# Two-block network on one core: the three engines' order of work in the twelve head pairs of the state-space scan

## The reference, cut to what matters

```python
def ssd_chunked(x, dt, A, B, C, h0):           # cut
    a_cum = jnp.cumsum(a, axis=-1)
    lmat = jnp.exp(segsum(a))                   # decay from token s to token l, one matrix a head
    cb = jnp.einsum('bclgn,bcsgn->bgcls', cc, bc)
    y_diag = jnp.einsum('bgcls,bgrcls,bcsgrp->bclgrp', cb, lmat, xc)
    ...
    y_off = jnp.einsum('bclgn,bcgrpn,bgrcl->bclgrp', cc, prev_states, jnp.exp(a_cum))
    y = (y_diag + y_off).reshape(bsz, length, g, r, p)

def ssd_mixer(...):                             # cut: forward and backward scan, skip, gate, norm by group
    y = y_f + flip(y_b) + d_skip * xs
    gated = y * jax.nn.silu(zs)
    gated = gated * lax.rsqrt(jnp.mean(gated * gated, axis=-1, keepdims=True) + EPS)

# beside it, for the second block: adaptive scales, shifts and gates from a conditioning vector
mods = jnp.split(silu_c @ ada_w[l] + ada_b[l], 6, axis=-1)
```

## Time and profile before

| | |
|---|---|
| three timed runs | 2001.25, 2004.65, 2007.44 us |
| profiled execution | 2007.44 us, span on the core 2005.4 us |
| PE busy | 1729.2 us, 86% of the span |
| DVE, ACT, POOL busy | 619.6, 356.7, 56.2 us |
| granted PE clock, mean | 0.945 of full speed |
| the twelve pairs | from 298.25 us (first `head_rows`) to 425.65 us (first product of `w_out0`), 127.4 us |

### The profile page before, as it was taken

The page is one execution under the profiler, slowest core; times in us unless marked ns, Lnnn a source line. Parts: engine busy times, 40 slices in busy tenths (PEclk is TensorE's granted clock), DMA queues, the critical chain, the costliest instruction groups (busy, mean ns, idle before and its releaser), DMA issues.

```text
span 2005.4 us, 23465 instructions
## 1 busy us (share of the span) xinstructions
PE 1729.2 (86%) x9806; PEld 881.8 (44%) x9806; DVE 619.6 (31%) x1405; ACT 356.7 (18%) x868; POOL 56.2 (3%) x51
## 2 busy tenths in 40 slices
PE   6999998899999998989999989889998766566664
PEld 3844674444444576433333323246574433233322
DVE  2157837633200485332222222140343101110101
ACT  2112226512101363100000000021441000000000
POOL 0000200020100000000000000000000000000000
PEclk9899998899999999999999999999999977888887
DMA  8241337786322103279999999941307999999996
GB/s 335 105 168 48 121 126 284 296 340 258 121 84 84 42 1 126 103 298 429 427 428 428 427 427 426 428 175 53 142 35 305 423 427 427 427 426 427 427 427 254
DMA packets 39100, 538.21 MB, mean 268 GB/s; under 512 B 4330, under 2 KB 4714, under 8 KB 6612
## 3 DMA queue, kind: packets, MB, share of 16 engines
q1 hardware_dynamic: 37860, 530.84, 63.9%
q0 software_dynamic: 1136, 5.88, 0.8%
HBM read 535.66 MB, written 1.05 MB: 268 GB/s over the span
## 4 chain that ended last, share of the span: by engine, by line
PE 58%; issue 25%; DMA 11%; DVE 5%; ACT 1%; DVEq 1%; POOL 0%; SPq 0%; POOLq 0%; ACTq 0%
PE bank L597 55%; DMA mem<-in_moe 8%; PE bank L607 2%; DVE mem L1326 1%; DMA mem<-in_w_ada 1%; DVEq L1323 1%; DMA mem<-in_w_out 1%; DMA mem<-in_ada_w 0%; POOL mem L2303 0%; DVE mem L1489 0%; DVE mem L1800 0%; ACT mem L2009 0%; DVE mem L1617 0%; ACT mem L1990 0%; DVE mem L1638 0%
## 5 line engine op out<-in xcount | busy, mean ns | idle before, releaser
L597 PE MATMUL bank<-mem 128*32 128x256 f32 (+12 forms) x8990 | 1612.5, 495 | 251.5 <-DMA mem<-in_moe 162.3
L597 PEld LDWEIGHTS bank<-mem 128*32 128x32 f32 (+4 forms) x8990 | 790.5, 150 | 1019.0 <-issue 715.4
L2009 ACT ACTIVATE mem<-bank 128x512 f32<-128x512 f32 (+3 forms) x285 | 142.5, 507 | 1096.7 <-PE bank L597 767.9
L1800 DVE TENSOR_TENSOR mem<-mem,bank 128x512 f32<-128x512 f32 (+1 forms) x32 | 17.7, 554 | 490.8 <-PE bank L597 490.8
L1817 DVE TENSOR_TENSOR mem<-bank,mem 32x512 f32<-32x512 f32 (+1 forms) x128 | 70.9, 554 | 227.3 <-PE bank L597 226.0
L607 PE MATMUL bank<-mem 128*128 128x128 f32 x760 | 120.3, 287 | 16.1 <-DVE mem L1800 5.2
L607 PEld LDWEIGHTS bank<-mem 128*128 128x128 f32 x760 | 88.3, 147 | 80.6 <-issue 46.7
L1463 DVE SCALAR_TENSOR_TENSOR mem<-mem 128x256 f32<-128x256 f32 x160 | 86.9, 543 | 9.6
L1990 ACT ACTIVATE mem<-mem 128x1024 f32<-128x1024 f32 x22 | 23.1, 1051 | 190.4 <-DVE mem L1557 147.4
L1326 DVE TENSOR_SCALAR mem<-bank,mem 128x128 f32<-128x128 f32 (+2 forms) x136 | 45.4, 405 | 35.5 <-PE bank L607 31.7
L1964 ACT ACTIVATE mem<-bank 128x256 f32<-128x256 f32 (+2 forms) x54 | 19.7, 396 | 169.9 <-PE bank L597 169.9
(11 more groups left out here) (181 smaller groups left out, 515.1 us busy)
## 6 DMA issues: line engine op xcount, KB each, us to landing
mem<-in_moe SPq DMA_DIRECT2D x192, 2048.0 KB, 34.9
mem<-in_ada_w SPq DMA_DIRECT2D x24, 2048.0 KB, 8.2
mem<-in_w_in SPq DMA_DIRECT2D x10, 2048.0 KB, 7.6
mem<-in_w_ada SPq DMA_DIRECT2D x6, 2048.0 KB, 12.3
mem<-in_even_w_in SPq DMA_DIRECT2D x6, 2048.0 KB, 10.2
mem<-in_w_out SPq DMA_DIRECT2D x4, 2048.0 KB, 8.9
mem<-in_odd_w_in SPq DMA_DIRECT2D x3, 2048.0 KB, 21.0
mem<-in_even_w_out SPq DMA_DIRECT2D x2, 2048.0 KB, 8.2
```

The costliest lines, as they stand in the source:

```text
L597: return nc.tensor.matmul(o, lhsT, rhs, start=start, stop=stop, skip_group_check=True)
L2009: took(name, S.activation(o, i, func))
```

## The change

The order in which PE, DVE and ACT take the steps of the twelve pairs is written anew. No instruction is added or removed, and no buffer is changed.

- PE: iteration m now ends with `pair_y(m)` instead of holding `pair_y(m - 1)` in its middle. The two `head_rows` of the next pair stand apart, each with one adaptive row behind it. `ada_outs` comes one row after its own row, where before it came an iteration later. Sums and group rows follow one iteration nearer.
- DVE: `pair_out(m - 1)` stands before the second `decay_args` and before `mixing(m)`, where before it stood behind `mixing(m)`. In the pairs that close a group (m = 5, 8, 11), `group_ms` stands ahead of both `decay_args`.
- ACT: a `take` of an adaptive row follows each `decays`, and `pair_squares(m - 1)` is last.

```diff
-            for m in range(HEADS // 2 + 1):
-
-                for h in (2 * m + 2, 2 * m + 3):
-                    if h < HEADS:
-                        head_rows(h)
-                if m:
-                    pair_y(m - 1)
-                if m >= 3:
-                    pair_sum(m - 3)
...
-                for k in pending:
-                    ada_outs(k)
-                pending = [ADA_AT_HEAD[h] for h in (2 * m, 2 * m + 1) if h in ADA_AT_HEAD]
-                for k in pending:
-                    ada_rows(k)
+            for m in range(HEADS // 2):
+                for h in (2 * m, 2 * m + 1):
+                    if h + 2 < HEADS:
+                        head_rows(h + 2)
+                    if h in ADA_AT_HEAD:
+                        ada_rows(ADA_AT_HEAD[h])
+                        if h:
+                            ada_outs(ADA_AT_HEAD[h] - 1)
+                pair_y(m)
+                if m >= 2:
+                    pair_sum(m - 2)
+                if m >= 5 and m % 3 == 2:
+                    group_rows((m - 5) // 3)
```

```diff
             for m in range(HEADS // 2):
-                for h in (2 * m + 2, 2 * m + 3):
-                    if h < HEADS:
-                        decay_args(h)
-                mixing(m)
+                closing = m >= 5 and m % 3 == 2
+                if m < 11 and not closing:
+                    decay_args(2 * m + 2)
                 if m:
                     pair_out(m - 1)
-                if m >= 5 and m % 3 == 2:
+                if closing:
                     group_ms((m - 5) // 3)
+                if m < 11 and closing:
+                    decay_args(2 * m + 2)
+                if m < 11:
+                    decay_args(2 * m + 3)
                 if m >= 6 and m % 3 == 0:
                     group_out((m - 6) // 3)
-                for k in pending:
-                    ada_outs(k)
-                pending = [ADA_AT_HEAD[h] for h in (2 * m, 2 * m + 1) if h in ADA_AT_HEAD]
+                mixing(m)
+                for h in (2 * m, 2 * m + 1):
+                    if h in ADA_AT_HEAD and h:
+                        ada_outs(ADA_AT_HEAD[h] - 1)
```

More of the change, by code:

```diff
@@ L840, in _ @@
             head_rows(1)
-            pending = []
-            for m in range(HEADS // 2 + 1):
-                for h in (2 * m + 2, 2 * m + 3):
-                    if h < HEADS:
-                        head_rows(h)
-                if m:
-                    pair_y(m - 1)
-                if m >= 3:
-                    pair_sum(m - 3)
[L851 to L854, removed]
-                for k in pending:
-                    ada_outs(k)
-                pending = [ADA_AT_HEAD[h] for h in (2 * m, 2 * m + 1) if h in ADA_AT_HEAD]
-                for k in pending:
-                    ada_rows(k)
+            for m in range(HEADS // 2):
[11 more added lines that the diff above has]
+                    group_rows((m - 5) // 3)
             for k in range(ADA_LEFT, 26):
@@ L2102, in _ @@
             for m in range(HEADS // 2):
[L2103 to L2107, removed]
                 for h in (2 * m, 2 * m + 1):
+                    if h + 2 < HEADS:
+                        decays(h + 2)
                     if h in ADA_AT_HEAD:
@@ L2111, in _ @@
                         take(f"row{k}", ada_row[k % 2], arrive(act, f"row{k}")[:, :])
+                if 1 <= m < 11:
+                    pair_squares(m - 1)
             pair_squares(10)
```

## The result

The changed kernel took 2037.13 us (median of 4 runs, 2029.6 to 2042.75) against 2005.22 us for the kernel before (4 runs). The ratio is 1.016 with a 95% interval of 1.0122 to 1.0196. It is slower by 31.9 us; 2034 was forecast, with a range of 2019 to 2050.

The account below looks back on a forecast made before the run. PE was taken to bound the kernel, the stage being 102.0 us of work plus waits and half clock. Waits +19.6 and clock +9.0 gave +28.6 us, 2034 forecast against the median, 80% range 2019 to 2050.

Parts of the forecast that it names:

- The fixed wait of an odd pair: In pairs 1, 3, 5, 7, 9 PE waits 3.9 us from second spread rows to y(m), 20.8 us with pair 9's `group_out`.
- The even pairs: In pairs 2, 4, 6, 8, 10 a row and an out cover part of the 3.9 us, leaving 4.7 us of waits.
- The spread rows of head 12: In iteration 5 they wait 0.9 us for a bank that `pair_out` and `group_ms` must free.
- Row 18's 0.4: In iteration 8 row 18 waits 0.4 us for a bank, part of 1.3 us in place of 7.2.
- Pair 0: Out 6 moves into the wait ahead of y0, which falls from 4.9 to 4.0 us.
- The wait for `w_out0`: At the stage's end PE's 1.0 us wait for this transfer goes, since the stage is slower.
- the second halves of y: The second half of each y waits 0.2 us for `c_dec_done` in ten pairs, 2.0 us.
- The clock: Half clock behind waits costs 6.2 us after the first and 3.0 after each odd pair's: 21.2, before 12.2.
- the short waits of the even pairs cost nothing beyond themselves: Clock step for even pairs: no clock loss behind short waits, as at the 1.02 us wait for `w_out0`.
- Its rival as I priced it: Clock stays low for long: half of the work behind y1 at half clock, +54 us, about 2058; chance 12%.
- the case of 2018 us: Rival: the waits come but the clock doesn't fall in odd pairs, +13.6 us, about 2018; chance 10%.
- The case of a mixing that isn't late: Rival: `m_ready` comes before PE reaches y(m), so only old waits and their clock go, about 1992; chance 3%.

Follow-up runs that it names:

- e2: The kernel before with the new order on DVE alone, PE and ACT as before; 1997.6 us, ratio 0.9963 to the kernel before.
- e5: The changed kernel with `mixing(m)` ahead of the arguments of head 2m+3 and of `group_out` on DVE; 2004.3 us, ratio 0.9979 to the kernel before.
- e3: The kernel before with `pair_out` and `group_ms` ahead of the mixing in pairs 5, 8 and 11 alone; 1997.1 us, ratio 0.9959 to the kernel before.
- e4: The changed kernel with four useless 128x512 products ahead of `pair_y` in pairs 1, 3, 5, 7 and 9; 2025.5 us.
- e1: The changed kernel with DVE back in the old order, except output and mean first in pairs that close a group; 2047.1 us.
- e7: The kernel before with early `pair_out` and `group_ms` in pairs 5, 8, 11, and pair 0's wait filled by rows and outs; 1994.2 us.

## Why the prediction was right

**The direction and the mechanism.** The chain over both engines, spread rows of head 2m+3, arguments, mixing, y(m), is what costs. The undo of PE and ACT (e2) takes the stage from 154.9 to 113.5 us, and moving the mixing past those arguments and `group_out` (e5) takes it to 123.0. The waits stand where the prediction put them.

**The fixed wait of an odd pair.** 3.9 us were worked out and 3.81 measured, four times the same. Pair 9 with `group_out` was to be 5.15 and is 4.99. The five sum to 20.2 us for 20.8.

**The even pairs.** 0.3, 1.3, 1.5, 1.3 and 0.3 were forecast; the profile has 0.97, 1.31 and 0.97 for pairs 4, 6 and 8, and none to be seen for 2 and 10: 3.3 us for 4.7.

**Banks, pair 0 and the end.** The spread rows of head 12 wait 0.64 us for 0.9. Row 18's 0.4 is not there. Pair 0 waits 4.50 us, for 4.0, and the parts of that sum were off. Out 6 began when it was to (10.3 us after the stage's start). But two spread rows that stood ahead of y0 now stand behind it, so PE came to the wait at 5.8 us and not 6.5. And out 6 at half clock took 1.6 us for 0.9, so that y0 followed it without a wait. The wait for `w_out0` went, but one of 0.56 us for the last group's bank took its place, which I had missed.

**The sum of the waits.** The listed ones are 20.2 + 3.3 + 0.6 + 4.5 + 0.6 = 29.2 us for 30.8 without the second halves of y. With 154.9 - 102.0 - 19.6 = 33.3 us for all that isn't work or clock, where 32.8 was forecast, some 4 us stand inside PE's busy time, y's second half among them.

**The clock.** 21.2 us were forecast and 19.6 measured, but the parts are not mine. The first wait cost 3.2 us and not 6.2 (1.4 in e2 and e3, where it is as long as before), and the five odd ones 1.7, 3.4, 1.3, 3.4 and 1.6, 11.4 for 15. In exchange the waits of 1.31 us (pair 6) and 0.97 us (pair 8) cost 1.7 and 3.4, where I had nothing for an even pair. The step that failed is "the short waits of the even pairs cost nothing beyond themselves", taken from one wait of 1.02 us; it was priced at nothing and measured 5.1 us. That the sum came within 1.6 us of 21.2 is luck: the first and the odd waits were 6.6 us too dear. The rule that I set against it, of the Trainium skill, "TensorE: Matmul & The Clock Gate", section on a second failure mode of the clock, describes such a case on another kernel: brief idling between groups lets the clock swing. By that rule this trace agrees for two of three such waits (the 0.97 us at 363.98 had no fall behind it). But the same waits don't always cost: in e4 the clock stayed up in pairs 6 and 8 and fell in pair 4, the other way round, and in e1 it was 1.00 behind the 0.97 us of pair 8. So no fixed price for a short wait comes out of these runs. Its rival as I priced it, half of all later work at half clock, did not come.

**The other rivals.** The clock fell behind all five odd waits, so the case of 2018 us is out. The case of a mixing that isn't late would have been 1992; e2 and e3, which have that property, came out at 1997.6 and 1997.1.

**The total.** +28.6 us were forecast and +27.5 measured in the stage; the medians differ by 31.9. The profile before, from which the forecast starts, lost 4.8 us more behind y0 than e2 and e3 did. With their loss in its place the stages would differ by some 32 us (an estimate, 27.5 + 4.8). How often the kernel before has the larger loss isn't known.

## What to carry to other kernels

When steps of several engines are interleaved by hand, count for each consumer the work that its own engine has between the step that starts the producer's chain and the wait, and compare it with that chain's length. A lag of one whole iteration hid here what a closer order exposed in eight of the eleven pairs behind the first. A step that has no part in the result but stands ahead of it on the producing engine (the arguments of the next head ahead of this pair's mixing) is as good as a dependency. And where a wait names an instruction whose result PE doesn't need, look for the bank: freeing it ahead of the mixing removed 6.5 us of waits here (4.11 + 3.10 - 0.73).

## What was unexpected in the hardware

The granted clock falls behind waits much shorter than the 3.10 us that I had as the shortest case. In e3 it was low behind a wait of 0.73 us that was followed by outs 12 and 13 and row 14 (the first line). The 8 spread rows behind them took 1.97 us, and the same work one pair later took 1.09:

```profile
343.42 4.23 PE L597 MATMUL bank<-mem 128*128 128x2 f32 x32 [0.73 <-DVE mem L1509]
347.58 1.97 PE L607 MATMUL bank<-mem 128*128 128x128 f32 x8
...
357.61 1.09 PE L607 MATMUL bank<-mem 128*128 128x128 f32 x8
```

In e7 it was low with no wait of PE in the timeline for 30 us before it, after outs and a row (the first two lines). e3 has the same work at the same place, and there the clock stayed up and the spread rows took 1.09 us and not 1.97 (the last two), so the kind of work alone doesn't decide it:

```profile
384.95 4.38 PE L597 MATMUL bank<-mem 128*128 128x2 f32 x32
389.26 1.97 PE L607 MATMUL bank<-mem 128*128 128x128 f32 x8
```

```profile
377.25 3.70 PE L597 MATMUL bank<-mem 128*128 128x2 f32 x32
380.88 1.09 PE L607 MATMUL bank<-mem 128*128 128x128 f32 x8
```

The stretches of e7 have, for the same place:

```profile
386.00:392.00 6.00, 6.00 (x40) 3.31 (x41) 5.55 (x17) 3.57 (x11) 0.00 (x0) 0.72 0.96 404
```

PE's busy share was 6.00 of 6.00 us there. So a PE that the profile shows busy doesn't always keep its clock. Nor does a long wait always cost the same: behind y0's 4.9 us the loss was 6.2 us before and 1.4 in e2 and e3. What decides it, the runs don't settle.
